# Retention steps between half slabs, two weight slabs at a time at five boundaries, and the embeddings transposed before the down projection

## The reference

```python
# first block
h = rms_norm(x, g_mix);  z = h @ w_in           # latent attention and gated linear attention
x = x + concat([attention, gla]) @ w_o
h = rms_norm(x, g_ffn)
x = x + (silu(h @ w_gate) * (h @ w_up)) @ w_down          # width 2816
gate = sigmoid(rms_norm(x, g_ple) @ w_ple_gate)
x = x + gate * (p @ w_ple_proj)                            # p: 512 x 256 embeddings
# second block
h = rmsnorm(x, g_pre_mix)
q, k, v, g, u, sv, a_ret, a_sgu = split(h @ w_in)
y_ret = (layernorm(retention(rotary(q), rotary(k), v)) * silu(g)) @ w_ret_o   # 4 heads, both directions
y_sgu = (gelu(u) * (w_spatial . layernorm(gelu(sv)) + b)) @ w_sgu_o
merged = sigmoid(a_ret) * y_ret + sigmoid(a_sgu) * y_sgu
x = x + rmsnorm(merged @ w_out, g_post_mix)
h2 = rmsnorm(x, g_pre_ffn)
x = x + rmsnorm(gated_conv_mlp(h2), g_post_ffn)            # width 2 x 2816, 3-tap convolution
```

## Time and profile before

| | |
|---|---|
| median of 3 runs | 1727.41 us (1726.53 to 1731.61) |
| the profiled execution | 1728.11 us, span 1726.8 us |
| mean granted TensorE clock | 0.979 of full speed |
| TensorE busy | 1646.0 us, 7857 matmuls |
| VectorE busy | 882.4 us |
| ScalarE busy | 653.7 us |

### The profile page before, as it was taken

How to read it: one execution, slowest core, us unless ns; L and a number is a source line. 1 busy time by engine, 2 the same in 40 slices (tenths; PEclk the granted TensorE clock), 3 DMA queues, 4 the chain that set the end, 5 groups by cost and what they waited for, 6 DMA issues and landing times.

```text
span 1726.8 us, 18642 instructions
## 1 busy us (share of the span) xinstructions
PE 1646.0 (95%) x7857; PEld 1355.8 (79%) x7857; DVE 882.4 (51%) x1168; ACT 653.7 (38%) x796; POOL 11.7 (1%) x25
## 2 busy tenths in 40 slices
PE   7999999999999999998999799999997899999997
PEld 6777677778888888776887698888875688888886
DVE  6556556564444422367526533354343777676323
ACT  4546667342222211254423233223232444444211
POOL 1000000000000000000000000000000000000000
PEclk9999999999999999998999999999998899999998
DMA  4321011123333232322321032212222132222221
GB/s 157 92 74 49 25 49 50 49 98 98 98 98 96 97 97 94 112 74 73 104 74 50 25 104 93 95 57 98 98 98 74 49 98 98 98 95 91 97 96 73
DMA packets 120274, 144.28 MB, mean 84 GB/s; under 512 B 6009, under 2 KB 109776, under 8 KB 120192
## 3 DMA queue, kind: packets, MB, share of 16 engines
q1 hardware_dynamic: 118768, 139.87, 24.7%
q0 software_dynamic: 1232, 3.16, 0.6%
q10 hardware_dynamic: 192, 0.07, 0.0%
HBM read 140.99 MB, written 2.10 MB: 83 GB/s over the span
## 4 chain that ended last, share of the span: by engine, by line
PE 91%; DVE 5%; ACT 2%; issue 1%; DMA 1%; SPq 0%; DVEq 0%; ACTq 0%
PE bank L364 27%; PE bank L366 27%; PE bank L365 27%; PE bank L826 1%; PE bank L585 1%; PE bank L584 1%; PE bank L603 1%; PE bank L651 1%; DVE slab_lo L948 1%; PE bank L809 1%; PE bank L632 1%; PE bank L874 1%; PE bank L402 1%; PE bank L646 0%; DVE tmp L961 0%
## 5 line engine op out<-in xcount | busy, mean ns | idle before, releaser
L364 PE MATMUL bank<-h_hi,slab_hi 128*128 128x512 f32 x1320 | 527.3, 399 | 20.5 <-DVE h_lo L953 10.4
L366 PE MATMUL bank<-h_hi,slab_lo 128*128 128x512 f32 x1320 | 519.3, 393 | 0.0
L365 PE MATMUL bank<-h_lo,slab_hi 128*128 128x512 f32 x1320 | 519.3, 393 | 0.0
L948 DVE TENSOR_TENSOR slab_lo<-slab_raw,slab_hi 128x2048 fp32r<-128x2048 f32 x130 | 296.0, 2278 | 326.7 <-ACT slab_hi L1634 326.4
L364 PEld LDWEIGHTS bank<-h_hi,slab_hi 128*128 128x128 f32 x1320 | 251.7, 191 | 81.9 <-issue 27.6
L1634 ACT ACTIVATE slab_hi<-slab_raw 128x2048 fp32r<-128x2048 f32 x130 | 246.3, 1896 | 152.5 <-DMA slab_raw<-in_w_down 142.8
L365 PEld LDWEIGHTS bank<-h_lo,slab_hi 128*128 128x128 f32 x1320 | 251.6, 191 | 53.9 <-issue 2.2
L366 PEld LDWEIGHTS bank<-h_hi,slab_lo 128*128 128x128 f32 x1320 | 251.0, 190 | 53.5
L987 DVE TENSOR_TENSOR tmp<-bank,x_rstd_rows 128x512 f32<-128x512 f32 x98 | 67.2, 687 | 110.7 <-PE bank L366 110.6
L364 PE MATMUL bank<-slab_hi,h_hi 128*128 128x256 f32 x320 | 91.5, 286 | 2.2 <-DVE slab_lo L948 2.2
L366 PE MATMUL bank<-slab_hi,h_lo 128*128 128x256 f32 x320 | 90.5, 283 | 0.0
(11 more groups left out here) (384 smaller groups left out, 1963.9 us busy)
## 6 DMA issues: line engine op xcount, KB each, us to landing
slab_raw<-in_w_in SPq DMA_DIRECT2D x40, 1024.0 KB, 4.9
slab_raw<-in_w_up SPq DMA_DIRECT2D x33, 1024.0 KB, 5.0
slab_raw<-in_w_down SPq DMA_DIRECT2D x22, 1024.0 KB, 4.9
slab_raw<-in_w_gate SPq DMA_DIRECT2D x11, 1024.0 KB, 5.1
slab_raw<-in_w_o SPq DMA_DIRECT2D x4, 1024.0 KB, 4.9
slab_raw<-in_w_ple_gate SPq DMA_DIRECT2D x4, 1024.0 KB, 5.2
slab_raw<-in_w_ret_o SPq DMA_DIRECT2D x4, 1024.0 KB, 4.9
slab_raw<-in_w_sgu_o SPq DMA_DIRECT2D x4, 1024.0 KB, 4.8
```

The lines of the kernel that those rows point to most:

```text
L364: T.matmul(ps, a_hi, b_hi, start=start, stop=False, skip_group_check=skip)
L365: T.matmul(ps, a_hi, b_lo, start=False, stop=False, skip_group_check=skip)
L366: return T.matmul(ps, a_lo, b_hi, start=False, stop=stop, skip_group_check=skip)
L948: V.tensor_tensor(w_lo[j][:, 0:n], raw[j][:, 0:n], w_hi[j][:, 0:n].bitcast(F32), ALU.subtract).then_inc(slab_lo, 1)
```

## The change

Seven parts, none of which alters what is computed:

- **Two slabs together** (`two_slabs`, `part`) after the norms of gate/up, pg and IN2 and at w_out: the first slab's input tiles 0 to 5, then the second's (tiles 0 to 2, sum of squares, tiles 3 to 5, spread), then tiles 6 and 7 of both. At UP2 the two slabs go tile by tile, and sum and spread lie in the third slab, which uses banks 4 and 5. The slabs' splits move ahead of the norm's steps on ScalarE and VectorE.
- **Embeddings**: p is transposed after gate/up pair 9; its DMA is issued after hid_lo tile 8 instead of the last; the split of PLE+1 lies between the additions of down. pg reads pg_hi/pg_lo, so that h_hi/h_lo of the next norm can be written during pg, tile by tile.
- **Retention** in eight steps, each with two half slabs (`half_tm`, `half_fm`) in banks 7 and 0 or 4: v slabs 1 to 3, the four g slabs, the first sv slab. `ret_outputs` comes two steps after `ret_prepare`, `ret_gated` four.
- **Spatial weights** behind the first two pairs of branch 1, their offsets computed after the third.
- **m_hi/m_lo**, the split of merged, is made during branch 2; the squares for the post norm are taken from PSUM by ScalarE, with the gain applied in the copy; three kinds of splits are placed between them.
- **UP2**: the first four outputs are scaled together; b2up 0 and 1 use tmp 6 and 7.
- **DOWN2**: four outputs instead of two are advanced before the last slab.

```diff
+        def two_slabs(g, names, hi, lo, ready, late, norm=None):
+            wv = []
+            for s in range(2):
+                T.wait_ge(slab_lo, g + s + 1)
...
+                for t in range(2):
+                    take(names[2 * s + t], 2 * ((g + s) % 2) + t)
+                if s == 0:
+                    part(wv, 0, names, hi, lo, 0, late, ready)
+            if norm is None:
+                part(wv, 1, names, hi, lo, 0, late, ready)
+            else:
+                i, sq = norm
+                part(wv, 1, names, hi, lo, 0, 3, ready)
+                norm_sum(i, sq, rot())
+                part(wv, 1, names, hi, lo, 3, late, ready)
+                norm_spread(i, rot())
+            for s in range(2):
+                part(wv, s, names, hi, lo, late, KT, ready)
+                slab_end[g + s] = state["whole"]
+
+        def part(wv, s, names, hi, lo, first, last, ready):
+            hv, lv = wv[s]
+            for n in range(2 * (last - first)):
+                k, t = first + n // 2, n % 2
+                if t == 0:
+                    T.wait_ge(ready[k][0], ready[k][1])
...
-        for n in range(FT // 2):
-            slab_fm(FF + 2 * n, [("gate", 2 * n), ("gate", 2 * n + 1)], ready=h_ready(1) if n == 0 else None)
-            if n == 0:
-                norm_rows(1)
+        two_slabs(FF, [("gate", 0), ("gate", 1), ("up", 0), ("up", 1)], *h_k, h_ready(1), 6, (1, tmp[0]))
+        for n in range(1, FT // 2):
+            slab_fm(FF + 2 * n, [("gate", 2 * n), ("gate", 2 * n + 1)])
             slab_fm(FF + 2 * n + 1, [("up", 2 * n), ("up", 2 * n + 1)])
+            if n == FT // 2 - 2:
+                T.wait_ge(p_landed, 16)
...
+        two_slabs(PLE + 1, [("pg", n) for n in range(4)], *pg_k, h_ready(2), 6, (2, x2[:, 0, :]))
+        for n in range(2, 4):
+            slab_fm(PLE + 1 + n, [("pg", 2 * n), ("pg", 2 * n + 1)], src=pg_k)
+        two_slabs(IN2, [("rot", n) for n in range(4)], *h_k, h_ready(3), 6, (3, x2[:, 0, :]))
...
+        for s in range(RET_SLABS):
+            if s < HEADS:
+                ret_prepare(s)
+            if 2 <= s < HEADS + 2:
+                ret_outputs(s - 2)
+            if 1 <= s <= HEADS:
+                ret_pairs(s - 1)
+            for t in range(2):
+                b = (7, 4 if s in (0, RET_SLABS - 1) else 0)[t]
+                if s < 3:
+                    half_tm(IN2 + 5 + s, ("v", s + 1, t), t, b)
+                elif s < 7:
+                    half_fm(IN2 + 5 + s, ("g", 2 * (s - 3) + t), t, b)
+                else:
+                    half_tm(SV, ("sv", 0, t), t, b, 0)
+                if t == 0 and s >= HEADS:
+                    ret_gated(s - HEADS)
...
+        for k in range(KT):
+            for s in range(2):
+                part(wv, s, names, *h_k, k, k + 1, h_ready(5))
...
+        part(wv, 0, [("a2", 2), ("a2", 3)], *h_k, 0, 1, h_ready(5))
+        norm_sum(4, x2[:, 0, :], 6)
+        part(wv, 0, [("a2", 2), ("a2", 3)], *h_k, 1, 3, h_ready(5))
+        norm_spread(4, 7)
+        part(wv, 0, [("a2", 2), ("a2", 3)], *h_k, 3, KT, h_ready(5))
...
-        for n in range(2):
-            down_tokens(0, n, range(FT - 6, FT - 2))
+        for n in range(TT):
+            down_tokens(n // 2, n % 2, range(FT - 6, FT - 2))
...
 # VectorE, pg
         for n in range(4):
+            if n:
+                split(PLE + 3 + n)
+                for k in range(2 * n - 2, 2 * n):
+                    norm_tile(3, k, "g_pre_mix_2")
+                sum_tiles(x2_k, squared, 2 * KT, 2 * n - 2, 2 * n)
             for t in range(2):
...
 # VectorE, retention
+        for s in range(RET_SLABS):
+            if s < HEADS:
+                ret_prepare(s)
+            split(IN2 + 6 + s)
+            if 2 <= s < HEADS + 2:
+                ret_means(s - 2)
+            if 1 <= s <= HEADS:
+                ret_state_updates(s - 1)
+            if 2 <= s < HEADS + 2:
+                ret_layernorm(s - 2)
...
 # VectorE, post norm and UP2
+                emptied(("o2", k))
+                scaled_step = step(V.tensor_tensor(w, o2[:, k, :], t.ps[:, :], ALU.mult))
             if k:
                 norm_tile(5, k - 1, "g_pre_ffn_2")
+            if k < KT:
+                V.wait_ge(vector_step, scaled_step)
+                V.tensor_tensor(xT[:, k, :], xT[:, k, :], w, ALU.add).then_inc(post_done, 1)
+        split(UP2 + 2)
+        sum_tiles(x2_k, squared, 3 * KT, 0, KT, squares_summed)
+        norm_rows(4)
+        for t in range(2):
+            scaled(("a2", t), tmp[4 + t])
+        for t in range(2):
+            scaled(("b2up", t), tmp[6 + t])
+        split(UP2 + 3)
...
+                if 2 * n + s2 == 2:
+                    split(UP2 + 4)
+                if 2 * n + s2 == 3:
+                    V.wait_ge(conv_right, 2 * n + 2)
+                if 2 * n + s2 > 3:
+                    split(UP2 + 2 * n + s2 + 1)
...
 # ScalarE, pg
+            if n:
+                split(PLE + 3 + n)
             for t in range(2):
                 f = 2 * n + t
                 emptied(("pg", f))
                 A.activation(tmp[f % 4], tmp[f % 4], ACT.Sigmoid).then_inc(ple_sigmoid, 1)
+                A.wait_ge(x_done, f + 1)
+                A.activation(h_hi[:, f, :], xT[:, f, :], ACT.Identity, scale=col("g_pre_mix_2", f)).then_inc(h_hi_done, 1)
+                A.activation(x2[:, f, :], xT[:, f, :], ACT.Square).then_inc(squared, 1)
...
 # ScalarE, w_out
+            t = tile["o2", k]
+            A.wait_ge(psum_ready, t.done)
+            A.activation(tmp[k], t.ps[:, :], ACT.Square).then_inc(post_squared, 1)
+            A.activation(o2[:, k, :], t.ps[:, :], ACT.Identity, scale=col("g_post_mix_2", k)).then_inc(t.free, 1)
...
 # GpSimd
-        G.wait_ge(hid_lo_done, FT)
+        G.wait_ge(hid_lo_done, KT)
         G.dma_start(p_tm[:, :, :], p[0, 0].rearrange("(t q) c -> q t c", q=P)).then_inc(p_landed, 16)
```

More of the change, by code:

```diff
@@ L755, in tensor_program @@
         down(DOWN, "down", hid_hi, hid_lo, hid_lo_done)
[L758 to L763, removed]
         T.wait_ge(slab_lo, PLE + 1)
@@ L797, in ret_prepare @@
             whole(("ret_kt", hd), ins)
-            tile["ret_s", hd].done = state["whole"]
+            ps = take(("ret_s", hd), 0)
+            for j in range(RC):
+                ins = T.matmul(ps[:, chunk[j]], k[:, chunk[j]], q[:, chunk[j]], start=j == 0, stop=True,
+                               skip_group_check=True)
+            whole(("ret_s", hd), ins)
         def ret_pairs(hd):
@@ L859, in branch @@
                 slab_fm(g0 + 2 * n + 1, [(name, "a", 2 * n), (name, "a", 2 * n + 1)])
+                if g0 == BR1:
+                    spatial_weights(n)
         branch(BR1, "b1", 0)
-        T.wait_ge(spatial_landed, 16)
-        ps = take("w_t", rot())
-        for g in range(GRP):
-            ins = T.transpose(ps[:, chunk[g]], w_sp[:, g, :], ident)
-        whole("w_t", ins)
-        T.wait_ge(tile["w_t"].free, tile["w_t"].value)
-        ps = take("w_rows", rot())
-        whole("w_rows", T.matmul(ps[:, :], ones, w_t, start=True, stop=True))
         T.wait_ge(sv_normed, TT)
@@ L879, in tensor_program @@
         branch(BR2, "b2", KT)
-        for n in range(4):
-            slab_fm(WOUT + n, [("o2", 2 * n), ("o2", 2 * n + 1)], ready=h_ready(4) if n == 0 else None)
-        def post_rows(i, banks):
-            T.wait_ge(post_summed, i + 1)
-            ps = take(("post_sum", i), rot(banks))
-            whole(("post_sum", i), sum_rows(ps[:, 0:TT], tmp[0], True, True))
-            T.wait_ge(post_diag, i + 1)
-            b = rot(banks)
-            ps = take(("post_row", i), b, post_done, KT)
-            whole(("post_row", i), T.matmul(ps[:, :], ones, tmp[1], start=True, stop=True))
@@ L892, in tensor_program @@
-        post_rows(0, (4, 5, 6, 7))
-        for n in range(FT // 2):
-            slab_fm(UP2 + 2 * n, [("a2", 2 * n), ("a2", 2 * n + 1)], ready=h_ready(5) if n == 0 else None)
-            if n == 0:
-                norm_rows(4)
+        two_slabs(WOUT, [("o2", n) for n in range(4)], *m_k, h_ready(4), 6)
+        for n in range(2, 4):
+            slab_fm(WOUT + n, [("o2", 2 * n), ("o2", 2 * n + 1)], src=m_k)
+        T.wait_ge(post_summed, 1)
+        ps = take("post_sum", 6)
+        whole("post_sum", sum_rows(ps[:, 0:TT], tmp[0], True, True))
@@ new lines, in tensor_program @@
+        T.wait_ge(post_diag, 1)
+        ps = take("post_row", 7, post_done, KT)
+        whole("post_row", T.matmul(ps[:, :], ones, tmp[1], start=True, stop=True))
+        names = [("a2", 0), ("a2", 1), ("b2up", 0), ("b2up", 1)]
+        wv = []
+        for s in range(2):
+            T.wait_ge(slab_lo, UP2 + s + 1)
+            wv.append([w[(UP2 + s) % RING][:, :].rearrange("p (k c) -> p k c", k=KT) for w in (w_hi, w_lo)])
+            for t in range(2):
+                take(names[2 * s + t], 2 * ((UP2 + s) % 2) + t)
@@ new lines, in tensor_program @@
+        for k in range(KT):
+            for s in range(2):
```

(11 more changed lines are left out.)

432 lines of the change are left out of this document (246 added, 186 removed).

## The result

The changed kernel takes 1670.43 us (median of 4 runs, 1669.57 to 1670.59) where the kernel before, on the same chip, takes 1729.16 (4 runs, 1726.53 to 1731.61): a ratio of 0.967, 95% interval 0.964 to 0.969. Forecast were 1675 us, 1657 to 1688. The profiled execution took 1669.57 us.

What follows compares the result with a forecast made beforehand. TensorE, busy 1646.0 of 1726.8 us, bounds the kernel; only idle time and low clock, at most 85.5 us, can be gained. Terms sum to 52.0: 1727.4 - 52.0 = 1675.4, rounded to 1675, range 1657 to 1688.

Steps and rivals of the forecast that it cites:

- low stretches: TensorE at half clock after waits: guessed costs 1.7, 3.5, 2.7 us and none twice; off by up to 6.
- the term of w_out and up: From w_out through the start of up: loss falls from 29.1 to 16.9 us, gain 12.2.
- The pg chain: Embeddings to second block: dependent ScalarE and VectorE steps take 14.1 us per pair against TensorE's 10.9; gain 1.4.
- Rival (a): At pg, ScalarE and VectorE overlap better, so their chain does not bind: 15.9 us less, 1659; chance 0.14.
- These two boundaries: Embeddings and entry of the second block: loss 17.3 us before, about 15.9 after, hence gain 1.4.
- The retention: Half slabs between all steps cover an 11.0 us chain with 13.7 us: loss 26.8 to 0.8, gain 26.0.
- Rival (c): Clock falls in the woven stretch, 3.4 us in each of eight steps, 14 us in all: 1689; chance 0.06.
- The start of up: After w_out TensorE still waits 1.6, 1.4, 3.1, 0.8 and 3.8 us, plus 3.5 and 2.7 for the clock.
- Rival (b): More waits than counted, above all at the start of up, and some bank waits: 1685; chance 0.13.
- First gate slab: Two slabs at once after the norm hide the wait for the diagonal: gain 1.4 us.
- spatial weights: Moved under the branch slabs, ending 2.5 us idle and 1.7 of low clock: gain 4.2 us.
- last down slabs: Four outputs ahead of the last slab cover a 3.76 us wait and its low clock: gain 6.8 us.

Runs made afterwards that it cites:

- e7: Changed kernel with both tiles of a pg pair scaled and through the sigmoid first, and ScalarE's IN2 and IN2+1 splits directly behind those sigmoids; 1656.97 us.
- the doses: Changed kernel with eight, or three, additional VectorE additions in each of four retention steps; 1679.0 us with eight, 1670.71 us with three.
- e12: Changed kernel with pg pairs reordered (sigmoids first, split behind them) and up's splits half a pair earlier, without filler matmuls; 1651.18 us.
- e11: Changed kernel with pg pairs reordered (sigmoids first, split behind them), up's splits half a pair earlier, and useless filler matmuls after w_out; 1648.09 us.
- e9: Changed kernel with useless filler matmuls put into TensorE's three waits after w_out; 1667.98 us.

## Why the prediction was right

It held because each term rested on a chain followed through rows, and the chains came out to within 0.3 us in most of their steps and 1 us at their ends. The sizes put down for low stretches were guesses (1.7 at the second block, 3.5 and 2.7 at up, none twice); that they came as 1.7, 3.2 and 3.1 is in part luck, for in a second profile of the same kernel the one after w_out cost 2.0 and the term of w_out and up was 15.0 us instead of 13.9. All terms erred to the same side or not at all, so no error hid another.

*The pg chain* was forecast with sigmoids at P+20.8 to P+65.8 and the end of IN2+1 at P+83.7. With P = 729.9, the end of proj, they start at 750.94 to 795.92 (P+21.0 to P+66.0) and IN2+1 ends at 812.6 (P+82.7). TensorE gets h_lo 4 at P+60.1 (forecast P+59.8) and the sum of squares at P+71.0 (forecast P+71.0), and waits, earlier, for banks:

```profile
767.19 0.47 PE L373 MATMUL bank<-pg_hi,slab_hi 128*128 128x512 f32 x1 [2.26 <-DVE tmp L1081]
781.45 0.47 PE L373 MATMUL bank<-h_hi,slab_hi 128*128 128x512 f32 x1 [3.13 <-DVE tmp L1081]
789.96 0.50 PE L373 MATMUL bank<-h_hi,slab_hi 128*128 128x512 f32 x1 [2.80 <-DVE h_lo L1044]
...
800.91 0.27 PE L422 MATMUL bank<-const_small_sb,residual_squares 128*128 128x1 f32 x1 [0.97 <-DVE residual_squares L1052]
```

Rival (a), that this chain does not bind, is refuted in the changed kernel; e7, which unbinds it, shows what it would have been worth: 14 us (15.9 forecast). The term was still too small, 1.4 instead of 3.4 us. The ends were right to 1 us; the step that failed is "These two boundaries lose 11.1 + 6.2 = 17.3 us now and about 15.9 after", a difference of two losses that are not counted alike: the first is idle time and low clock as they stand in the rows, the second the distance to a time without waits that is itself an estimate. The difference of the two ends, 99.0 us before (820.1 less 721.1) less 0.9 for the transposes against 10.9 + 83.7 + 0.65 after, would have said 2.8.

*The retention* came out at 27.1 for 26.0. Idle time is 1.0 us (0.8 forecast: two waits of 0.49 for bank 0, as named). TensorE's busy time fell by 7.6, where the clock had been priced at 6.3; that is the rest, and what the other 1.3 us of busy time are is not shown. The margin of 11.0 against 13.7 us was real at its tightest place, 2.7 us, by the doses. Rival (c) fell: the clock stayed at 1.00 in the changed kernel and in the retention alone. What stands between the slabs' matmuls are ten pieces, from eight transposes in 1.0 us to 8.8 us of plain float32 products with four transposes (0.6 us) ahead of them, so not transposes between all halves as the rival has it:

```profile
874.97 0.60 PE L853 MATMUL bank<-const_small_sb,ret_qk 128*128 128x128 f32 x4
...
927.77 1.04 PE L894 MATMUL bank<-const_small_sb,tmp 128*128 128x128 f32 x8
```

The Trainium skill (TensorE: Matmul & The Clock Gate, Part 4) says that transposes do not count as busy in the way that other matmuls do. With at most 1.0 us of them at a time no run here shows whether that is so.

*The start of up.* Forecast waits 1.6, 1.4, 3.1, 0.8 and 3.8 us; measured 1.41, 1.29, 3.14, 0.17 and 3.56. The low stretches there, as windows of TensorE (busy us, clock), the last row being that of the entry of the second block:

```profile
1281.90:1292.10 10.20, 6.33 (x12) 0.50 0.15 52
1350.20:1357.00 6.80, 6.11 (x14) 0.50 0.22 76
790.40:793.80 3.40, 3.40 (x10) 0.50 0.00 0
```

Half of the busy part is 3.2, 3.1 and 1.7 us, forecast 3.5, 2.7 and 1.7. The loss after is 9.6 us of waits and 6.2 of clock, 15.8 for the 16.9 forecast, which is 1.1 of the 1.7 by which the term came out larger (13.9 for 12.2). Rival (b) did not occur.

*First gate slab, spatial weights, last down slabs* are within 0.1 us each. In all 56.9 of the 58.6 us belong to the change, 4.9 more than summed, most of it (2.0, 1.1, 1.7) in the three terms with low stretches.

## What to carry to other kernels

- Follow each chain instruction by instruction with its rows, and take the gain as the difference of the two end times; a loss against an ideal time carries the error of the ideal into a small term.
- Where an engine at half load sets the pace, look at its order before its work: what the next stage needs (here the second sigmoid, and the split) goes ahead of what only a later one needs (h_hi, squares). Two such swaps gave 13.7 + 6.7 us by stages, about a third of what the whole change gave, with no instruction of the three compute engines more or less; in the medians e12 is 17 to 19 us below the changed kernel.
- A wait is worth more than its length where TensorE is otherwise dense (3.8 us gave 6.9, 3.6 gave 6.7), since a low stretch went with it; but filling a wait with useless matmuls gives little where another engine paces TensorE afterwards (1.1 to 2.7 us, and 2.3 in e11 against e12).

## What the runs showed of the hardware

- The same program has its low-clock stretches at different places from one execution to the next: at the entry of the second block one of 3.4 us in the first profile of the changed kernel, two in the second (781.1 and 794.8). The stage took 116.4 and 116.7 us: where a chain of other engines binds, a low stretch costs almost nothing.
- A low stretch lengthens what stands alone too: the spread of the post norm's row took 2.08 us in the changed kernel and 1.12 in e9, and the first matmul of up came 1.0 us sooner after the end of w_out.
